# Attention by heads: values stationary, probabilities of two tiles moved past them, in an encoder layer on one core

## The reference, cut to what matters

```python
q = rope_2d(rms_norm(q.reshape(B, L, 8, 64), q_norm), row, col)
k = rope_2d(rms_norm(k.reshape(B, L, 2, 64), k_norm), row, col)
...
s = einsum('bkgqd,bksd->bkgqs', qblk, kt) * scale     # 4 tiles of 128 queries, 8 heads
p = softmax(s, axis=-1)                               # over 512 keys
o = einsum('bkgqs,bksd->bkgqd', p, vt)
...
y = concatenate([group_rms_norm(y_hy, g_hy, 8), group_rms_norm(y_at, g_at, 8)], axis=-1)
x = x + y @ w_out
```

## Time and profile before

| | |
|---|---|
| median of 3 executions | 804.81 us (804.64 to 807.08) |
| the profiled execution, its own time | 806.54 us |
| its span in the profile | 804.7 us |
| TensorE busy, of the span | 763.3 us (95%), 3844 matmuls |
| VectorE busy | 605.0 us (75%) |
| ScalarE busy | 460.6 us (57%) |
| GpSimd busy | 74.0 us (9%) |
| mean granted TensorE clock | 0.988 |
| DMA | 146.54 MB, mean 182 GB/s |

### The profile page before, as it was taken

One profiled execution on the slowest core, in us unless ns is written; L12 is line 12 of the kernel. 1 busy time (PEld: TensorE's weight loads), 2 busy tenths in 40 slices (PEclk: granted clock), 3 DMA queues, 4 the chain that ended last, 5 costly groups with the idle time before them and its releaser, 6 DMA issues.

```text
span 804.7 us, 11166 instructions
## 1 busy us (share of the span) xinstructions
PE 763.3 (95%) x3844; PEld 623.3 (77%) x3844; DVE 605.0 (75%) x929; ACT 460.6 (57%) x677; POOL 74.0 (9%) x86
## 2 busy tenths in 40 slices
PE   5899999999999899989997998999999999999994
PEld 3764858788898799978785696788888888888873
DVE  5478383997799778834447568899998999998882
ACT  5754252231244867622359342688878888888873
POOL 0000000000000000000000001112222323222001
PEclk9999999999999999999999898999999999999998
DMA  8720202130130020012221466899999999999841
GB/s 290 290 79 26 79 26 79 35 97 1 31 101 27 10 96 2 1 53 79 78 79 53 152 260 259 330 417 361 364 373 376 384 388 369 371 371 383 325 169 20
DMA packets 28543, 146.54 MB, mean 182 GB/s; under 512 B 4791, under 2 KB 6711, under 8 KB 21976
## 3 DMA queue, kind: packets, MB, share of 16 engines
q1 hardware_dynamic: 23320, 135.53, 44.8%
q0 software_dynamic: 5184, 10.50, 4.9%
HBM read 141.81 MB, written 12.58 MB: 192 GB/s over the span
## 4 chain that ended last, share of the span: by engine, by line
PE 71%; DVE 14%; ACT 6%; DMA 6%; issue 2%; SPq 1%; POOL 0%; POOLq 0%; DVEq 0%; ACTq 0%
PE bank L1846 15%; PE bank L1908 13%; PE bank L2274 10%; PE bank L2276 10%; PE bank L2275 10%; PE bank L1853 4%; DMA slot<-in_w_down 2%; PE bank L1920 2%; PE bank L2269 2%; DMA x_in<-in_x 1%; ACT pr L935 1%; DVE w_lo L1105 1%; PE bank L2188 1%; PE bank L2186 1%; PE bank L2187 1%
## 5 line engine op out<-in xcount | busy, mean ns | idle before, releaser
L1765 DVE TENSOR_TENSOR e_lo<-slot,e_hi 128x1024 fp32r<-128x1024 f32 x192 | 221.6, 1220 | 11.2 <-ACT e_hi L985 11.1
L985 ACT ACTIVATE e_hi<-slot 128x1024 fp32r<-128x1024 f32 x192 | 188.3, 1060 | 12.3 <-PE bank L2276 4.3
L1105 DVE TENSOR_TENSOR w_lo<-w_raw,w_hi 128x1024 fp32r<-128x1024 f32 x41 | 49.5, 1223 | 75.3 <-ACT w_hi L688 75.1
L688 ACT ACTIVATE w_hi<-w_raw 128x1024 fp32r<-128x1024 f32 x41 | 42.7, 1063 | 101.6 <-DMA w_raw<-in_w_in 63.6
L2274 PE MATMUL bank<-e_hi,hgT_hi 128*128 128x512 f32 x240 | 95.0, 396 | 0.3 <-DVE hgT_lo L1777 0.3
L2276 PE MATMUL bank<-e_hi,hgT_lo 128*128 128x512 f32 x240 | 93.7, 390 | 0.0
L2275 PE MATMUL bank<-e_lo,hgT_hi 128*128 128x512 f32 x240 | 93.4, 389 | 0.0
L2274 PEld LDWEIGHTS bank<-e_hi,hgT_hi 128*128 128x128 f32 x240 | 45.2, 189 | 9.8 <-DVE hgT_lo L1777 0.7
L2276 PEld LDWEIGHTS bank<-e_hi,hgT_lo 128*128 128x128 f32 x240 | 45.1, 188 | 9.6
L2275 PEld LDWEIGHTS bank<-e_lo,hgT_hi 128*128 128x128 f32 x240 | 45.1, 188 | 8.8
L2274 PE MATMUL bank<-e_hi,gaT_hi 128*128 128x512 f32 x120 | 48.1, 401 | 0.0
(11 more groups left out here) (393 smaller groups left out, 1716.1 us busy)
## 6 DMA issues: line engine op xcount, KB each, us to landing
slot<-in_w_down SPq DMA_DIRECT2D x16, 2048.0 KB, 17.9
slot<-in_w_gate SPq DMA_DIRECT2D x16, 2048.0 KB, 16.4
slot<-in_w_up SPq DMA_DIRECT2D x16, 2048.0 KB, 17.5
w_raw<-in_w_in SPq DMA_DIRECT2D x18, 512.0 KB, 3.6
w_raw<-in_w_out SPq DMA_DIRECT2D x8, 512.0 KB, 3.7
w_raw<-in_w_k_mem SPq DMA_DIRECT2D x4, 512.0 KB, 6.3
x_in<-in_x SPq DMA_DIRECT2D x4, 512.0 KB, 9.2
w_raw<-in_w_v_mem SPq DMA_DIRECT2D x4, 512.0 KB, 6.1
```

Of the source, the lines that this page charges most:

```text
L688: act.activation(w_hi[ring(m)][:], w_raw[ring(m)][:], ACT.Copy).then_inc(s_wh, 1)
L985: act.activation(e_hi[buffer(b, j)][:], slot[slot_][:, 1024 * part:1024 * (part + 1)], ACT.Copy).then_inc(s_ehi, 1)
L1105: dve.tensor_tensor(w_lo[slot_][:], w_raw[slot_][:], w_hi[slot_][:].bitcast(F32), ALU.subtract)\
L1765: dve.tensor_tensor(e_lo[slot_][:, at_], slot[slot_][:, at_], e_hi[buffer(b, j)][:].bitcast(F32), ALU.subtract)\
```

## The change

A step's tile and head change roles: tile s % 4, head s // 4, so a head's four tiles follow each other. For two tiles at a time (`pv(j)`, after each odd step) the values of a head's group, high and low parts side by side (128 columns of `v_split`), are stationary, and the high, then the low parts of the probabilities of both tiles (256 columns) move past them: eight products in place of 24. The bank `O` of a head then holds high and low results by 64 rows over 512 tokens. ScalarE copies it (`out_copy`, at s % 4 == 0), TensorE transposes it back (`out_T`, at s % 4 == 2, a new job `OT` in bank 6 or 7), ScalarE copies the high columns (`out_first`, same step), VectorE adds the low ones (`out_sum`, same step), and squares and sums them (`out_squares`, a step later). The product of the low values and the low probabilities is now in the sum too.

Two q tiles are transposed ahead of the loop, the other six in steps 1, 3, 5, 7, 9, 11, the key tiles of the second group in steps 2 and 4; TensorE's job and ScalarE's copy of a tile have the same step number. Weight pieces 26, 27 are split in steps 10 to 13 instead of ahead of the loop, piece 28 in 14 and 15. The q sum of squares, its root and the exp table load move behind the key transposes. At the front, `hT` comes ahead of the last piece of `mk`, the 20 constant products go, the sine moves behind the splits of `hT`, and VectorE negates `w3`.

```diff
+QT_STEPS = [1 + 2 * h for h in range(NQ - 2)]
+KT_STEPS = [2, 4]
...
-    jobs += [("mk", j) for j in range(MT)] + [("hT", 0, k) for k in range(KT)] + filt(0, range(4))
+    jobs += [("hT", 0, k) for k in range(KT)] + [("mk", j) for j in range(MT)] + filt(0, range(4))
...
+            elif j[0] == "mk":
+                b = 6 + j[1]
+            elif j[:2] == ("hT", 0):
+                b, turn = j[2] % 6, 0
...
+        def column(s):
+            return NQ * (s % TT) + s // TT
+        def pair_half(buf, s):
+            return buf[:, s // 2 % 2, :, (s % 2) * P:(s % 2 + 1) * P]
+        def out_head(h):
+            return att[:, :, h * HD:(h + 1) * HD]
```

At ScalarE, the front:

```diff
+            for k in range(3):
+                split_hi(("hT", 0, k), hT_hi[:, k, :], col("norm_mix", k))
+            weight_hi(3, 1)
+            for k in range(3, KT):
+                split_hi(("hT", 0, k), hT_hi[:, k, :], col("norm_mix", k))
             act.wait_ge(s_arg, 2)
             act.activation(a2[0:FF, :], mlp_arg[:], ACT.Sin)
...
-            weight_hi(3, 1)
```

At ScalarE, ahead of the loop and in it:

```diff
-            for h in range(4):
-                qT_evac(h)
+            qT_evac(0)
+            head_rms(240, TT * NQ, HD, 3)
+            act.activation(small[:, 398:399], eps, ACT.Exp)
+            qT_evac(1)
...
+            def out_copy(h):
+                act.wait_ge(s_asq, 2 * h + 2)
+                if h >= 2:
+                    wait_filled(act, ("OT", h - 2))
+                free(act.activation(oT[:, h % 2, :], bank(("O", h))[:], ACT.Copy), ("O", h))
+            def out_first(h):
+                wait_filled(act, ("OT", h))
+                act.activation(out_head(h), bank(job)[:].rearrange("p (i w) -> p i w", i=TT)[:, :, 0:HD], ACT.Copy).then_inc(s_ohi, 1)
...
-                if s + 5 < NQ:
-                    qT_evac(s + 5)
+                if s in KT_STEPS:
+                    kT_evac(2 + KT_STEPS.index(s))
+                if s in QT_STEPS:
+                    qT_evac(2 + QT_STEPS.index(s))
+                if s % TT == 0 and s > 0:
+                    out_copy(s // TT - 1)
+                if s % TT == 2 and s > TT:
+                    out_first(s // TT - 1)
...
-                if s == MK_STEP + 3:
-                    weight_hi(28, 1)
+                if s in (10, 12, 14):
+                    weight_hi(26 + (s - 10) // 2, 1)
```

At VectorE:

```diff
-            weight_lo(26, 1)
...
-            weight_lo(27, 1)
...
+            def out_sum(h):
+                dve.wait_ge(s_ohi, h + 1)
+                free(dve.tensor_tensor(out_head(h), out_head(h), bank(job)[:].rearrange("p (i w) -> p i w", i=TT)[:, :, HD:2 * HD], ALU.add), job)
+            def out_squares(h):
+                wait_freed(dve, ("OT", h))
+                link(dve.tensor_tensor(o_sq[:], out_head(h), out_head(h), ALU.mult))
+                link(dve.tensor_reduce(small[:, 340:372].rearrange("p (i h) -> p i h", h=NQ)[:, :, h], o_sq[:], AX.X, ALU.add))
...
+                if s in (11, 13, 15):
+                    weight_lo(26 + (s - 11) // 2, 1)
+                if s % TT == 2 and s > TT:
+                    out_sum(s // TT - 1)
+                if s % TT == 3 and s > TT:
+                    out_squares(s // TT - 1)
```

At TensorE:

```diff
-            chunk_jobs("mk", memT_hi, memT_lo, split=lambda k: ("memT", k // 2),
-                       filler=(last_piece["mk"], ("hT", 0, 0), 20))
+            chunk_jobs("mk", memT_hi, memT_lo, part=slice(0, 3), split=lambda k: ("memT", k // 2))
             hT_jobs(0, x_in, lambda k: pe.wait_ge(s_xn, TT))
+            chunk_jobs("mk", memT_hi, memT_lo, part=slice(3, 4), split=lambda k: ("memT", k // 2))
...
-            def pv(s):
-                for k in range(4):
-                    pairs += [(pT_hi[:, s % NPR, tile_], v_hi[:, k, v0:v0 + HD]), (pT_hi[:, s % NPR, tile_], v_lo[:, k, v0:v0 + HD]),
-                              (pT_lo[:, s % NPR, tile_], v_hi[:, k, v0:v0 + HD])]
+            def pv(j):
+                for k in range(4):
+                    v_ = v_split[:, k, h // 4].rearrange("p w d -> p (w d)")
+                    pairs += [(v_, pT_hi[:, j % 2, k, :]), (v_, pT_lo[:, j % 2, k, :])]
+                ins = accumulate(job, bank(job)[:, 2 * P * half:2 * P * (half + 1)], pairs)
+            def out_T(h):
+                wait_freed(pe, ("O", h))
+                transposes(("OT", h), [oT[:, h % 2, i * P:(i + 1) * P] for i in range(TT)])
...
                 if s + 2 < NSEQ:
                     pt(s + 2)
+                if s % TT == 2 and s > TT:
+                    out_T(s // TT - 1)
+                if s in KT_STEPS:
+                    kT_job(2 + KT_STEPS.index(s))
+                if s in QT_STEPS:
+                    qT_job(2 + QT_STEPS.index(s))
...
-                if s >= 0:
-                    pv(s)
+                if s >= 0 and s % 2 == 1:
+                    pv(s // 2)
             for j in range(2, TT):
                 output_tile(wo0 + 1, j)
+            out_T(NQ - 1)
```

More of the change, by code:

```diff
@@ L88, in psum_jobs @@
     for s in range(-2, n):
-        if s >= 0 and s % NQ == 0:
-            jobs += [("O", s // NQ)]
+        if s >= 0 and s % TT == 1:
+            jobs += [("O", s // TT)]
         if s + 2 + AHEAD < n:
@@ L848, in gqa_exp @@
                     wait_filled(act, ("PT", s - NPR))
-                c0 = 240 + s
-                free(act.activation(pr[:, s % NPR, :], bank(("S", s))[:], ACT.Exp, bias=small[:, 100 + s:101 + s],
-                                    scale=small[:, c0:c0 + 1],
-                                    accum_out=small[:, 140 + s:141 + s]), ("S", s))
+                c0 = column(s)
+                free(act.activation(pr[:, s % NPR, :], bank(("S", s))[:], ACT.Exp, bias=small[:, 100 + c0:101 + c0],
+                                    scale=small[:, 240 + c0:241 + c0],
+                                    accum_out=small[:, 140 + c0:141 + c0]), ("S", s))
             def gqa_pt_hi(s):
@@ L882, in _ @@
                     hyena_root()
-                if s == MK_STEP + 3:
-                    weight_hi(28, 1)
-                if s % NQ == 3 and s > NQ:
-                    out_square(s // NQ - 1)
+                if s in (10, 12, 14):
+                    weight_hi(26 + (s - 10) // 2, 1)
             act.activation(small[:, 398:399], eps, ACT.Sqrt)
-            out_square(TT - 1)
+            out_copy(NQ - 1)
+            out_first(NQ - 1)
             head_rms(340, TT * NQ, HD, 4, floor=0.0)
@@ L1365, in keys_roped @@
                 dve.wait_ge(s_rope, 4)
-            dve.wait_ge(s_qsq, TT)
             for i in range(TT):
                 wait_freed(dve, ("q", i))
-            link(dve.tensor_reduce(small[:, 240:272], q_sq[:].rearrange("p i (h d) -> p (i h) d", d=HD), AX.X, ALU.add))
-            weight_lo(26, 1)
             roped(0, 0)
@@ L1390, in _ @@
             roped(2, 0)
-            dve.tensor_copy(small[0:1, 396:397], small[0:1, 240:241]).then_inc(s_ms, 1)
             q_split_lo(0)
@@ L1402, in _ @@
             q_split_lo(3)
+            dve.wait_ge(s_qsq, TT)
+            dve.tensor_reduce(small[:, 240:272], q_sq[:].rearrange("p i (h d) -> p (i h) d", d=HD), AX.X, ALU.add).then_inc(s_ms, 1)
+            for c in range(CT):
+                skipped(1, c)
             dve.wait_ge(s_hrms, 3)
             dve.reciprocal(small[:, 240:272], small[:, 240:272]).then_inc(s_qinv, 1)
-            for c in range(CT):
-                skipped(1, c)
             def hyena_inverse():
@@ L1470, in _ @@
                     mk_normed(s - MK_STEP)
-                if s == MK_STEP + 4:
-                    weight_lo(28, 1)
-                if s % NQ == 4 and s > NQ:
-                    link(out_sums(s // NQ - 1))
+                if s in (11, 13, 15):
[4 more added lines that the diff above has]
+                    out_squares(s // TT - 1)
                 if s - 2 in HR_STEPS:
@@ L1479, in _ @@
             link(dve.tensor_tensor(small[:, 140:172], small[:, 140:172], small[:, 140:172], ALU.mult))
-            link(out_sums(TT - 1))
+            out_sum(NQ - 1)
+            out_squares(NQ - 1)
             dve.scalar_tensor_tensor(small[:, 340:372], small[:, 140:172], EPS * HD, small[:, 340:372], ALU.mult, ALU.add)\
@@ L2038, in _ @@
             pe.wait_ge(s_qlo, TT)
-            for h in range(4):
+            for h in range(2):
                 qT_job(h)
```

107 lines of the change are left out of this document (49 added, 58 removed).

## The result

The changed kernel takes **845.46 us** (median of four runs, 842.79 to 849.43) against 805.72 for the kernel before beside it: a ratio of **1.0487, interval 1.0460 to 1.0514**, 39.7 us slower. The forecast was 824.2 with a range of 811 to 838. The sign is right, the size is about half of what came, and the range missed it.

What follows compares the result with a forecast made beforehand. TensorE was taken to bound the loop before (busy 77 of 80 us). Loop, start and tail +22.7, lost clock +1.7, front -5.0 make +19.4 us; on the median of 804.81 that gives 824.2, range 811 to 838.

Steps and rivals of the forecast that it cites:

- The value products: Loop: eight wide products per two steps cost 0.96 us instead of 2.67 for 24, saving 27 us of TensorE in all.
- The ring: Loop: in-order queues wait for each other from one exponential to the next; loop 95.5 us against 72.4, 23 longer.
- against it, that the wide products are dense: Loop: argument that dense wide products speak against TensorE's clock falling to 1.2 GHz; that case had chance 0.20.
- the low clock in the loop: Rival in the loop: TensorE, idle half its time, drops to 1.2 GHz; kernel 830 to 843 us, chance 0.20.
- +6 over a third of the steps, +19 over all: Loop: microseconds added if transposes at 1.2 GHz take 0.5 to 0.9 more a step; kernel 830 to 843.
- the list of steps: Loop: worked-out lengths of steps 0 to 28, in stretches of 23.2, 36.7 and 35.7 us, together 95.5.
- the bank wait of part 2: Loop steps 7 to 12: hyena sums wait for a bank the next exponential frees; steps 8 to 13 take 3.5 to 5.7.
- The front: Before the attention: transposes of h fill a wait, filters start at 35.6 instead of 40.56, gain 5.0 us (3 to 5.5).
- The start of the loop: Ahead of the loop: q sum and two weight splits moved; third exponential at 265.7 instead of 266.99, gain 1.3 us.
- The tail: Last exponential to the attention's transposes: 20.7 us against 19.8, first tile 1.4 after it; lost clock there 1.7 more.
- The faster rival: Loop: two-step lookahead swallows the waits, VectorE's work sets the pace at 72 us; kernel 795.6, chance 0.13.
- The signs: Loop and front: observations that would confirm the forecast, including 3.7 us output steps, TensorE under 75% busy, filters at 35.6.

Runs made afterwards that it cites:

- experiments 4 to 6: Changed kernel with: TensorE's side transposes ahead of the probabilities' (832.75 us); tile copies one step later (828.56); these and the turned output's copy, sum and squares later (816.42).
- experiment 3: Changed kernel plus identity products ahead of the scores in steps 1 to 7 and 14 to 18, ahead of the sums in 8 to 13; 839.97 us.
- experiment 2: Changed kernel plus five identity products ahead of the scores in steps 1 to 18; 844.46 us, ratio 1.0451.
- Experiment 8: Changed kernel with late copies, TensorE's side jobs ahead of the probabilities' transposes, and side jobs spread over the steps; 804.80 us, ratio 0.9969.
- experiments 11 and 12: Four, not six, projection tiles ahead of last value products: changed kernel with late copies, side jobs first and spread, 798.51 us; kernel before with new front, 800.79 us.

## Why the prediction was right in sign and short in size

**The value products** are as priced: in the changed loop at full clock they follow each other at (267.67 - 266.76)/7 = 0.13, with the 0.120 of the earlier trace rows between most of them.

```profile
266.76 0.36 PE L1887 MATMUL bank<-pT_hi,v_split 128*128 128x256 f32 x1
...
267.67 0.28 PE L1887 MATMUL bank<-pT_lo,v_split 128*128 128x256 f32 x1
```

By the formula of the Trainium skill (TensorE: Matmul & The Clock Gate, section Back-to-back issue gap) the distance is 109 ns for 256 columns and 29 for 64; for 256 the rows come near it, for 64 they showed 0.111 us before. The section itself calls this the gap of an isolated product, which at small N leaves out the weight load, so the prediction read it too narrowly. The rows of the loads before bear that out: each narrow product brings its own load of 128 columns, and the loads too start 0.11 apart.

```profile
271.88 0.19 PEld L1846 LDWEIGHTS bank<-v_hi,pT_hi 128*128 128x128 f32 x1
271.99 0.19 PEld L1846 LDWEIGHTS bank<-v_lo,pT_hi 128*128 128x128 f32 x1
```

The weight loads were busy 71.59 of 80 us in the loop before. So the change does save TensorE's work, as part 1 said, and what it saves is sixteen products of each pair's 24 together with their loads. That the load sets the 0.111 fits these rows; no run tested it apart.

**The ring** is what the prediction said, and experiments 4 to 6 show it by taking it apart: the same instructions in other places of the queues give back up to 29 us. The full-clock steps bear the list out where it could be seen at once: step 1 3.02 (3.0), 2 3.61 (3.6), 22 3.72 (3.7), 23 2.31 (2.3), 24 3.25 (3.3), 27 4.17 (4.2), 28 1.72 (1.7).

**The step that failed first** is "against it, that the wide products are dense", by which the low clock in the loop got a chance of 0.20 and no place in the forecast's sum. It was the largest missing term: some 9 to 13 us (experiment 3), at 0.53 to 0.54 of the clock from 272 to 290 and from 300 to 335 us. "+6 over a third of the steps, +19 over all" brackets it, but in part by luck, since the price of a step was too low: "transposes on the ring take 0.5 to 0.9 more a step" stands against 1.33 for a step with scores, probabilities and a tile on the ring (5.39 less 4.06). It left out the scores, which take 1.02 instead of 0.55. What I did not see is that my own ring, in which TensorE mostly waits for the other two engines, makes the loop a stage like the one before 440 us. The Trainium skill's rule (TensorE: Matmul & The Clock Gate, Part 1), that the gate opens with activity and closes in idleness, was set beside it as agreeing only with the stage before 440 us. It held in the loop: with products added in the idle time the clock was 1.00 from 270 to 290, without them 0.54 from 272 to 290.

**The step that failed second** is the list of steps itself, short by up to 8.5 us at full clock. Steps 3 to 5 were priced 11.2 and are 12.7. The square of 0.5 on ScalarE was in the price; the score products were not. In these steps their bank comes free only with the step's exponential, so they stand ahead of the probabilities' transposes (272.74 and 273.31 behind the exponential of 271.81 in experiment 2), 0.5 a step. It is the bank wait of part 2, written out there for the sums alone. Step 14 was priced 3.9: its output transposes stand behind the hyena sums and a value product as in step 10, which I had costed there and not here; without filler it is 6.02 - 1.03 = 5.0. For output steps I put the transposes of s+2 at 0.95 behind the exponential. That holds where the value products of the step before are done by then (step 22, 3.72). In step 18 they start only with the exponential (333.56 against 333.61 in the third filler run), and it is 5.30 - 1.03 = 4.3 instead of 3.7; step 26 is 4.62. One error went the other way: step 17 was priced 2.6 and is 1.39.

**The front** was forecast 5.0 and gave 3.7 at the filters. The list ahead of the sine (eight copies, a table load, two passes) left out the weight piece that ScalarE splits among the copies:

```profile
27.87 3.65 PE L1894 MATMUL bank<-ident,x_in 128*128 128x128 f32 x32
...
30.23 1.06 ACT L712 ACTIVATE w_hi<-w_raw 128x1024 fp32r<-128x1024 f32 x1
...
36.82 1.13 PE L1961 MATMUL bank<-w_sum,a 128*128 128x512 f32 x2 [1.20 <-ACT a L770]
```

That is 1.06 of the 1.2 us. Another 0.7 is gone by the k transposes, which start 3.0 earlier; where was not tried. **The start of the loop** gave 0.6 more instead of 1.3.

**The tail** was right to half a microsecond: 21.1 us for 20.7, and the first tile 1.35 behind the last exponential for 1.4. That the lost clock came out at the 1.7 put on it is luck: it was the middle of 0 to 3.4.

**The faster rival**, that the lookahead swallows the waits, was wrong for this order of the queues. Experiment 8 takes 804.8 where it would have given 795.6. There VectorE's first maximum starts at 259.73 and the first projection tile at 338.12, 78.4 us where the rival had 72, so even in a good order VectorE's work alone does not set the loop. The rest lies in a front that gave less than 5.0 and in the tail.

**The signs** asked for: exponentials 3.7 apart in steps 6, 18, 22, 26 (4.25, 5.74, 3.72, 4.62), TensorE under 75% busy (71% from 262 to 355), filters at 35.6 (36.82), last exponential near 356 (379.22). The second came true and says nothing of the clock. The last one, and steps 6, 18 and 26 of the first, say that the loop had been sized wrong.

## What to carry to other kernels

An engine made faster inside a ring of in-order queues gained nothing here until the ring was opened, and then at most about 2 us (experiments 11 and 12), because the other engines' work was close behind it (VectorE busy 62.47 of 74 us in experiment 8). To open the ring, copy a side job's result one step after the step that makes it, and issue side jobs ahead of the work that waits for this step's result. When such a change leaves TensorE idle for a good part of each step, cost each of its operations on the ring at half clock as well, and put that into the sum, not among the rivals. A filler to keep the clock belongs ahead of the wait in which TensorE idles; a place behind it puts it on the path.

## What was not expected of the hardware

The busy share of TensorE does not tell its clock. From 300 to 335 us the changed kernel shows TensorE busy 25.80 of 35 us at 0.53 of the clock (103 matmuls, in the second group of rows above); the version with spread side jobs has the same busy time at full clock with 177:

```profile
300.00:335.00 35.00, 25.95 (x177) 21.03 (x176) 29.84 (x64) 25.76 (x55) 1.90 (x1) 1.00 0.01 1
```

At half clock the operations last longer and fill the idle time, so a kernel in this state looks nearly as busy as a healthy one. The granted clock beside the number of matmuls shows it.
